# A Hybrid Decoder Block on One Core: VectorE Turns the Second Norm's Rows in 32x32 Squares, Four Rows to a Store

## The reference

```
h    = rmsnorm(x);  proj = h @ w_in                     # 1024 -> 2048
yA   = rg_lru(conv4(proj_A)) * gelu(proj_gA)            # 512 channels
yB   = silu(layernorm(conv31(v * sigmoid(g))))          # 512 channels
x    = x + concat(rmsnorm(yA), rmsnorm(yB)) @ w_out     # "x2"
h    = rmsnorm(x) * norm_ffn                            # the second norm, "h2"
f    = silu(h @ w_gate) * (h @ w_up)                    # 1024 -> 2816
x    = x + f @ w_down
out  = rmsnorm(x) * norm_final
```

## Time and profile before

| | |
|---|---|
| median of 3 runs | 1904.94 us (1904.26 to 1905.03) |
| profiled execution | span 1902.7 us; the profile gives no time of it besides the span |
| TensorE busy | 1875.1 us, 99% |
| VectorE, ScalarE, GpSimd busy | 58%, 42%, 60% |
| DMA engines busy on queue 1 | 44.8% |

### The profile page before, as it was taken

One profiled execution on the slowest core, in us unless ns is written; L12 is line 12 of the kernel. 1 busy time (PEld: TensorE's weight loads), 2 busy tenths in 40 slices (PEclk: granted clock), 3 DMA queues, 4 the chain that ended last, 5 costly groups with the idle time before them and its releaser, 6 DMA issues.

```text
span 1902.7 us, 22499 instructions
## 1 busy us (share of the span) xinstructions
PE 1875.1 (99%) x8374; PEld 1544.2 (81%) x8374; DVE 1106.6 (58%) x1269; ACT 808.4 (42%) x938; POOL 1144.9 (60%) x427
## 2 busy tenths in 40 slices
PE   9999999999999999999999999999999999999998
PEld 7888788877788788888888788888888888888886
DVE  6899988997645755455545854445443025433535
ACT  6466766585643533333333433333333222232235
POOL 3577477945734465666655755555555676676663
PEclk9999999999999999999999999999999999999999
DMA  6222132265777334533355433323333765655455
GB/s 196 78 79 88 45 100 78 75 224 172 247 240 231 117 125 127 153 119 127 112 153 176 151 105 114 106 88 105 115 105 127 288 225 190 210 189 211 166 198 221
DMA packets 240946, 284.20 MB, mean 149 GB/s; under 512 B 12095, under 2 KB 166207, under 8 KB 240364
## 3 DMA queue, kind: packets, MB, share of 16 engines
q1 hardware_dynamic: 240874, 283.25, 44.8%
q10 hardware_dynamic: 2, 0.00, 0.0%
HBM read 200.90 MB, written 82.31 MB: 149 GB/s over the span
## 4 chain that ended last, share of the span: by engine, by line
PE 82%; POOL 6%; DVE 5%; ACT 2%; issue 2%; DMA 2%; POOLq 0%; SPq 0%; DVEq 0%; ACTq 0%
PE ps L2133 19%; PE ps L2135 19%; PE ps L2134 19%; PE acc L2133 8%; PE acc L2135 8%; PE acc L2134 8%; DVE a_lo L1863 1%; POOL nsq L877 1%; PE ps L2161 1%; DVE t_sum L1887 1%; POOL nsq L879 1%; POOL w_lo L804 1%; POOL f_lo L1018 0%; DVE wo_lo L1707 0%; POOL glu L827 0%
## 5 line engine op out<-in xcount | busy, mean ns | idle before, releaser
L933 POOL TENSOR_TENSOR t_lo<-t_sum,t_hi 128x2048 fp32r<-128x2048 f32 x44 | 205.6, 4674 | 165.3 <-ACT t_hi L1366 165.2
L927 POOL TENSOR_TENSOR b_lo<-m_raw,b_hi 128x1536 fp32r<-128x1536 f32 x44 | 157.6, 3582 | 179.2 <-ACT b_hi L1361 121.9
L1018 POOL TENSOR_TENSOR f_lo<-f_raw,f_hi 128x2048 fp32r<-128x2048 f32 (+1 forms) x42 | 182.2, 4338 | 129.3 <-ACT f_hi L1518 124.8
L2133 PE MATMUL ps<-h_hi,w_hi 128*128 128x512 f32 x512 | 201.1, 393 | 0.8 <-POOL w_lo L804 0.8
L2135 PE MATMUL ps<-h_hi,w_lo 128*128 128x512 f32 x512 | 199.4, 389 | 0.0
L2134 PE MATMUL ps<-h_lo,w_hi 128*128 128x512 f32 x512 | 199.2, 389 | 0.0
L1887 DVE TENSOR_TENSOR t_sum<-m_raw 128x512 f32<-128x512 f32 x88 | 141.7, 1630 | 97.4 <-PE acc L2135 87.6
L1518 ACT CAST f_hi<-f_raw 128x2048 fp32r<-128x2048 f32 (+1 forms) x42 | 74.3, 1769 | 263.6 <-PE ps L2135 168.1
L2133 PE MATMUL ps<-wd_hi,f_hi 128*128 128x512 f32 x462 | 179.8, 389 | 0.8 <-POOL wd_lo L1025 0.8
L2134 PE MATMUL ps<-wd_lo,f_hi 128*128 128x512 f32 x462 | 179.7, 389 | 0.0
L2135 PE MATMUL ps<-wd_hi,f_lo 128*128 128x512 f32 x462 | 179.7, 389 | 0.0
(11 more groups left out here) (257 smaller groups left out, 4689.1 us busy)
## 6 DMA issues: line engine op xcount, KB each, us to landing
f_raw<-f_scr SPq DMA_DIRECT2D x35, 1024.0 KB, 4.9
wd_raw<-in_w_down SPq DMA_DIRECT2D x60, 512.0 KB, 6.6
f_scr<-fs SPq DMA_DIRECT2D x110, 256.0 KB, 2.1
m_raw<-in_w_gate SPq DMA_DIRECT2D x88, 256.0 KB, 3.9
m_raw<-in_w_up SPq DMA_DIRECT2D x88, 256.0 KB, 5.1
w_raw<-in_w_in SPq DMA_DIRECT2D x32, 512.0 KB, 5.3
f_scr<-gt SPq DMA_DIRECT2D x44, 256.0 KB, 2.0
xt<-in_x SPq DMA_DIRECT2D x16, 512.0 KB, 6.3
```

Of the source, the lines that this page charges most:

```text
L927: g.tensor_tensor(b_lo[b][:, :, :, :], m_raw[b][:, 0:3], f32(b_hi[b][:, :, :, :]), ALU.subtract).then_inc(s_mlo, 1)
L933: g.tensor_tensor(t_lo[b][:, :, :, :], t_sum[b][:, :, :, :], f32(t_hi[b][:, :, :, :]), ALU.subtract).then_inc(s_mlo, 1)
L1018: g.tensor_tensor(f_lo[j % 3][:, 0:n], f_raw[j % 2][:, 0:n], f32(f_hi[j % 3][:, 0:n]), ALU.subtract).then_inc(s_dlo, 1)
L2133: pe.matmul(bank, lhs[0](c), rhs[0](c), start=first, stop=False, skip_group_check=more)
```

## The change

VectorE transposes `hn` in 32x32 squares into `turned[g]`, for a group of four row tiles, so that a square's row holds 4 x 32 positions (512 bytes) when the group is full. A square stays on its 32 partitions; the store puts it in its place: 16 DMAs of 32 partitions each (a block of positions t, a block of features q). Within a block of 512 the positions of `h2_scr` then stand in another order (32 of each of the four row tiles), and the x2 loads and the output stores undo it, four DMAs of 32 partitions in place of one (`pieces`). Groups 0, 1 and 2 are stored in steps 7, 9 and 12. The last group is stored in two halves of two row tiles, with runs of 256 bytes: `store_last(0)` in step 14, `store_last(1)` in SyncE's first iteration of the FFN, ahead of `store_f`. VectorE turns rows 14 and 15 at the end of matrix 1, behind `f_sum(1)`. TensorE's transposes and ScalarE's copies go; with banks 6 and 7 free, the outputs of rows from 2 on go round in six banks. `hn` has four buffers for the first rows. Loads of the FFN operands, sums and casts come a step later (`LOAD_AT` 10, `SUM_AT` 12 and 13); GpSimd's program is the same.

```
-        TURNED = {3: (0, 1), 4: (2, 3)}
+        TURN_AT = {4: (0, 1), 5: (2,), 6: (3, 4), 7: (5,), 8: (6, 7)}
+        STORE_GROUP_AT = {7: 0, 9: 1, 12: 2}
-        LOAD_AT, SUM_AT = 9, (11, 12)
+        LOAD_AT, SUM_AT = 10, (12, 13)
...
+        def out_bank(w, e):
+            return ps[e] if w < 2 else ps[(6, 7, 0, 1, 2, 3)[(4 * (w - 2) + e) % 6]]
...
+            def store_group(g):
+                h, st = divmod(g, NS)
+                sp_.wait_ge(s_turned, GROUP * (g + 1))
+                for t in range(SQS):
+                    for q in range(SQS):
+                        sp_.dma_start(h2_scr[h, q * SQ:(q + 1) * SQ, :, st * TILE + t * P:st * TILE + (t + 1) * P],
+                                      turned[g][t * SQ:(t + 1) * SQ].rearrange("j (k q) s -> j k q s", q=SQS)[:, :, q]
+                                      ).then_inc(s_h2st[g], 16)
+            def store_last(half):
+                n = P // 2
+                sp_.wait_ge(s_turned, NT - 2 + 2 * half)
+                for t in range(SQS):
+                    first = (NS - 1) * TILE + half * 2 * P + t * n
+                    for q in range(SQS):
+                        sp_.dma_start(h2_scr[NH - 1, q * SQ:(q + 1) * SQ, :, first:first + n],
+                                      turned[3][t * SQ:(t + 1) * SQ].rearrange("j (k q) s -> j k q s", q=SQS)[:, :, q]
+                                      ).then_inc(s_h2st[3], 16)
...
                 for i in range(QUADS[-1] + 2 if h == 0 else 0):
                     next_matrices(h, i, i)
+                    if i == 0:
+                        store_last(1)
...
                     store_f(h, i, i)
...
             def load_x2(t):
-                sp_.dma_start(x2[t][:, :], x2_scr[t]).then_inc(s_x2ld[(t // 4) % 2], 16)
+                for n, (w, r) in enumerate(pieces(t)):
+                    sp_.dma_start(x2[t][n * SQ:(n + 1) * SQ, :], x2_scr[w, r:r + SQ]).then_inc(s_x2ld[(t // 4) % 2], 16)
...
+            def store_columns(t, cols):
+                for n, (w, r) in enumerate(pieces(t)):
+                    sp_.dma_start(outr[w][r:r + SQ, cols], x2[t][n * SQ:(n + 1) * SQ, cols]).then_inc(s_ost, 16)
...
-                if 5 <= w < NT - 1:
-                    h2_copy(w - 1)
...
+                if n == 2:
+                    dve.wait_ge(s_h2st[2], STORED)          # first_half_sum
...
+            def row_turned(w):
+                g, r = divmod(w, GROUP)
+                if w >= NT - 2:
+                    dve.wait_ge(s_h2st[3], STORED)
+                if g == NT // GROUP - 1:
+                    r = r % 2
+                dve.wait_ge(s_hn, w + 1)
+                v.transpose(turned[g][:, :, r * SQ:(r + 1) * SQ], hn[hb(w)][:, :].rearrange("p (b i) -> p b i", i=SQ)
+                            ).then_inc(s_turned, 1)
...
                 if b and not late:
                     f_sum(0, i, h, first and h == 0)
                     f_sum(1, i, h, first and h == 0)
+                    if first and h == 0:
+                        row_turned(NT - 2)
+                        row_turned(NT - 1)
...
-                for turned in TURNED.get(w, (w - 1,) if 5 <= w < NT - 1 else ()):
-                    turn_h2(turned)
...
-                if n in (4, 5):
-                    turn_h2(NT - 6 + n)
```

More of the change, by code:

```diff
@@ L129, in hybrid_block @@
         w_raw = [at(f"w_raw{s}", [P, 2, KD, P], F32, o * KIB) for s, o in enumerate((128, 136, 200, 208))]
-        h2t = [at(f"h2t{s}", [P, KD, P], F32, (136 + 4 * s) * KIB) for s in range(2)]
+        turned = [at(f"turned{g}", [P, D // SQ, TILE // SQS], F32, o * KIB) for g, o in enumerate((184, 128, 88))]
+        turned += [at("turned3", [P, D // SQ, TILE // SQS // 2], F32, 136 * KIB)]
         uw = [at(f"uw{n}", [P, HALF], F32, o * KIB) for n, o in enumerate((144, 184))]
@@ L301, in hybrid_block @@
         s_xr = [sem(f"residual_loaded{n}") for n in range(4)]
-        s_tr = [sem(f"turned{b}") for b in range(2)]
         s_std2 = sem("std2_ready")
         s_hn = sem("hn_ready")
-        s_h2c = sem("h2_copied")
-        s_h2st = [sem(f"h2_stored{n}") for n in range(2)]
+        s_turned = sem("squares_turned")
+        s_h2st = [sem(f"h2_stored{g}") for g in range(4)]
         s_x2st = [sem(f"x2_stored{n}") for n in range(2)]
@@ L418, in from_sbuf, with hb, pieces @@
             return m, nd[m][:, :, first * P:(first + 1) * P]
+        def hb(w):
+            return w if w < 4 else w % 2
+        def out_bank(w, e):
+            return ps[e] if w < 2 else ps[(6, 7, 0, 1, 2, 3)[(4 * (w - 2) + e) % 6]]
+        def pieces(t):
+            block, a = divmod(t, GROUP)
+            if block < NT // GROUP - 1:
+                return [(GROUP * block + r, SQ * a) for r in range(GROUP)]
+            return [(GROUP * block + 2 * (a // 2) + r, SQ * (2 * (a % 2) + n)) for n in range(2) for r in range(2)]
         def decay_of(u):
@@ L642, in _ @@
                     store_x2(w - 1)
-                for turned in TURNED.get(w, (w - 1,) if 5 <= w < NT - 1 else ()):
-                    store_h2(turned)
                 if 2 <= w < NT - 2:
                     load_residual(w + 2)
+                if w in STORE_GROUP_AT:
+                    store_group(STORE_GROUP_AT[w])
+                if w == NT - 2:
+                    store_last(0)
                 if w == LOAD_AT:
-                    for n in range(2):
-                        sp_.wait_ge(s_h2st[n], 16 * TPH // 2)
+                    for g in range(NS):
+                        sp_.wait_ge(s_h2st[g], STORED)
                     sp_.wait_ge(s_out[3], TPH)
@@ L1117, in norm_swish @@
                     y_split(between)
-                if turned is not None:
-                    h2_copy(turned)
                 act.wait_ge(s_ysw, NJ * (m + 1))
@@ L1374, in _ @@
                     row_std(1)
-                    norm_swish(1, between=DIRECT[1], turned=0)
-                    h2_copy(1)
+                    norm_swish(1, between=DIRECT[1])
                 if 4 <= w < NT - 1:
@@ L1475, in gate_block @@
                 if starts == 0:
-                    h2_copy(NT - 2)
                     a_high(6)
@@ L1482, in gate_block @@
                 sums_hi(m + 1, 1)
-                if starts == 0:
-                    h2_copy(NT - 1)
                 silu(i, 1, h)
```

77 lines of the change are left out of this document (33 added, 44 removed).

## The result

The changed kernel takes 1927.88 us (median of 4 runs, 1926.68 to 1931.79), the kernel before 1904.72 in the same series: ratio 1.0124, 95% interval 1.0109 to 1.0139, so 23.2 us slower. The forecast was 1917.4 with a range up to 1926.0: the direction was right, the size was not, and the time lies 1.9 us outside the range. The profiled execution is the slowest of the four: 1931.79 us, span 1930.0.

The account below looks back on a forecast made before the run. The prediction took TensorE, busy 99% of the span, as the bound. Its terms, -3.1 + 1.6 + 10.0 + 1.6 + 2.4 = +12.5 us, on 1904.9 gave 1917.4 us, range 1905.5 to 1926.

Parts of the forecast that it names:

- TensorE's transposes: Output projection: removing 128 transposes saves 0.89 us a row, plus 1.3 us of waits, 15.5 us at most.
- Turns 14 and 15: Rows 14 and 15 are turned between products that wait for `a_lo` anyway, so removing their TensorE transposes gains nothing.
- the terms for rows 0 to 8: Output projection: rows 0 to 3 bring row 8 forward by 4.9 us; rows 4 to 6 give nothing.
- its 1.6 us of clock: Time lost to a lowered TensorE clock behind each of two new waits: 1.6 us each, bounds 0 and 3.2.
- the two new waits: TensorE waits 8.0 us for `y_lo` ahead of row 15 and 10 us for `sum11` at matrix 2.
- Row 15: Output projection: operands loaded a row later make TensorE wait 8.0 us for `y_lo(15)`, bounds 6.5 and 9.5.
- The DMA side "at nothing": Group stores and operand loads around rows 8 to 12 cost nothing; the last load lands some 12 us ahead of the sums.
- VectorE's turns: Added transposes on VectorE take 1.285 us a row, bounds 1.0 and 2.5; fourteen lie in its idle time.
- Matrix 2: First FFN loop: `store_last(1)` ahead of operand 3's store delays `sum11`; TensorE waits 10 us, bounds 5.8 and 16.6.
- The rival that 256-byte runs cost twice: Ahead of operand 3, 256-byte stores take 29 us in place of 9.7, +19 more: 1937; chance 0.07.
- The x2 loads: Down projection: x2 loads in fours lie ahead of loads that wait for GpSimd anyway; no cost was added.
- The end: The final row tile's output goes out in fours, adding 2.4 us, bounds 1.5 to 4.3.

Follow-up runs that it names:

- the other bank order: The changed kernel with its six output banks going round as 2, 3, 0, 1, 6, 7 instead of 6, 7, 0, 1, 2, 3: ratio 1.0097, 5.1 us less.

## Why the prediction was wrong, by its steps

- **TensorE's transposes.** 0.89 us a row is what rows 9 to 14 gain, within 0.04. Turns 14 and 15 gain nothing, as forecast. *The step that failed:* "So row 8 starts earlier only by what went before 496.19: 4 x 0.89 + 1.3 = 4.9 us." It took the four rows as free of other waits. Row 2's first product now uses bank 6, which ScalarE's root of the norm frees (`out_bank_free`, n = 0), a wait of 2.44 us that the diff shows in one line and the forecast never priced. With its clock it puts row 3 2.1 us late, and the chain up to `y_lo(8)` with it: row 8 starts 3.9 us ahead of the kernel before. With the other bank order it starts 8.2 ahead, so the terms for rows 0 to 8 were too low by 3.3 (0.6 of it a wait for `row` ahead of row 3 in the kernel before, which six banks remove; the rest was not taken apart). That 3.9 lies near 4.9 is luck: two errors cancel.
- **The clock behind row 8's wait.** A term was missing here too. The forecast had the wait ahead of row 8 grow, but added its 1.6 us of clock to the two new waits alone. In the changed kernel's trace the clock fell behind this wait as well (windows, the first three lines), and row 9 starts 3.2 us ahead, not the 5.8 that the terms give: 1.0 of the difference lies ahead of row 8, 1.7 behind. In the trace with the other bank order (the last line) the clock stayed full behind a wait of 3.06 us, and row 9 starts 9.0 ahead.

```profile
524.00:526.00 2.00, 1.25 (x3) 1.06 (x4) 2.00 (x1) 0.00 (x0) 0.69 (x1) 0.70 1.03 280
526.00:528.00 2.00, 2.00 (x6) 1.51 (x6) 2.00 (x3) 0.00 (x0) 0.00 (x0) 0.50 0.91 217
528.00:530.00 2.00, 2.00 (x10) 1.64 (x9) 1.57 (x4) 1.77 (x4) 0.00 (x0) 0.94 0.89 206
...
522.00:524.00 2.00, 2.00 (x10) 1.67 (x9) 2.00 (x4) 0.03 (x1) 0.00 (x0) 1.00 0.89 211
```

- **Row 15.** The mechanism was right, and one line of the diff makes it. The terms were low: `b_hi` ended 9.0 us behind row 13's products, not 7.5, since row 13's root waited for that row's adds, and these for two sums that held VectorE for 5.54 us. The forecast took 1.1 us off for the two copies that go; but in the kernel before, too, row 12's root started behind the adds and not behind the copies:

```profile
590.90 1.06 ACT L1351 ACTIVATE junk<-row 128x1024 bf16<-128x1024 f32 x1 [0.36 <-DVE row L1729]
```

`b_lo` took 5.48 us, not 3.50. The wait was 10.3 us, not 8.0; the clock behind it 2.5, not 1.6.
- **The DMA side "at nothing".** The load of row 15's y stands behind 13.3 us of group stores. In the changed kernel this is hidden by the casts that stand ahead of `y_hi(15)`; once they are moved, it is the next to be late.
- **VectorE's turns.** 1.24 us against the 1.285 taken; the estimate from the Trainium skill's figure, 2.5, is off by twice.
- **Matrix 2.** 10.5 us against 10.0, issues at 0.61 us against 0.617, clock 1.7 against 1.6. The rival that 256-byte runs cost twice fell: sixteen such stores held SyncE 10.3 us, as many runs of 512 bytes 13.3. Two bounds of this term were worked out wrongly: sixteen issues of 0.38 us give a wait of 6.3 us, not 5.8, and the upper one, 16.6, starts at 676.4, without the 1.9 us by which the sums had just been put earlier. Neither moves the forecast.
- **The second half's start.** Not in the forecast: +2.6 us. It is a collision that the kernel before meets or misses by its clock.
- **The x2 loads.** *The second step that failed:* "The x2 loads in fours lie ahead of loads that wait for GpSimd anyway." It put them at nothing; they cost 1 to 5 us, by what the pieces do to the DMA engines and not by their issue. It also did not look at how full they were. In the kernel before:

```profile
1500.00:1540.00 40.00, 40.00 (x178) 33.11 (x178) 10.28 (x16) 13.00 (x10) 31.89 (x11) 1.00 0.90 336
```
- **The end.** +2.7 against +2.4.

Between the forecast's +12.5 us and the trace's +27.3 lie 14.8: 2.7 for TensorE's later arrival at row 15's wait (1.0 ahead of row 8, 1.7 of clock behind it), 3.2 for that wait and its clock, 0.6 at matrix 2, 2.6 at the second half's start, 5.2 in the down projection, 0.3 at the end, and 0.2 of roundings. The median is 4 us lower than the trace; that the down projection, whose loss varies most from trace to trace, is the place was not shown.

## What to carry to other kernels

When a buffer rotation is changed, write down for each of its first uses which wait releases it, and when; the steady state tells nothing of it. A DMA had three prices here: its issue on the queue (which holds back all that is behind it), the time of the data, and its shape, which set how fast the engines moved it; where their share was near 1, pieces of 32 partitions cost even when another queue issued them. Price the clock behind every wait that grows, not behind the new ones alone. And mend the longest waits first, but look at what binds behind them: of 12 us gained ahead of the FFN here, 4 reached matrix 1.

## What the hardware showed that was not expected

- With the DMA engines at full share (1.04 and 1.06), a stretch with the x2 loads in pieces of 32 partitions by 4 KB moved 298 GB/s in all, with the same loads in 128 partitions by 1 KB 373.
- One DMA with 4 as its outermost size on the DRAM side ran at 92 to 104 GB/s, on a quarter of the engines.
- Behind nearly the same wait, 2.40 and 2.45 us, the granted clock was 0.52 in one trace and 1.00 in another, and the trace with the full clock lost more time.
- VectorE's 128x512 sum beside GpSimd's `b_lo` took 3.98 us in place of 0.68, and ended 0.55 us behind it; a wait added on GpSimd saved 5 us. The Trainium skill (GPSIMD Engine Reference, Specifications) names the SBUF interfaces that GpSimd shares with VectorE for instructions with two SBUF inputs; both are such, and the trace agrees.
